# Two attention loops on one Trainium2 core: probability copies cut in half between VectorE and ScalarE, and three steps moved in the order of the engines

## What is computed

```python
for i in range(DEPTH):                                   # DEPTH = 2
    n = rmsnorm(h, attn_norm_g[i])
    m = dsa_mixer(n, ...) if i % 2 == 0 else chunk_band_mixer(n, ...)
    h = h + m @ w_out[i]
    h = h + conv_ffn(rmsnorm(h, ffn_norm_g[i]), ...)

# inside both mixers, per head and block of queries
logits = q @ k.T * scale + bias        # masked keys are -inf
p = softmax(logits)
o = p @ v
```

## Time and profile before

| | |
|---|---|
| median of 3 executions | 3011.78 us |
| lowest and highest | 3011.35 and 3015.06 us |
| the profiled execution | 3010.81 us |
| its span, first to last instruction | 3008.6 us |
| mean granted clock of TensorE | 0.973 |
| TensorE busy | 2792.0 us, 93% |
| VectorE busy | 1525.4 us, 51% |
| ScalarE busy | 1111.2 us, 37% |
| GpSimd busy | 840.1 us, 28% |

### The profile page before, as it was taken

One profiled execution on the slowest core, in us unless ns is written; L12 is line 12 of the kernel. 1 busy time (PEld: TensorE's weight loads), 2 busy tenths in 40 slices (PEclk: granted clock), 3 DMA queues, 4 the chain that ended last, 5 costly groups with the idle time before them and its releaser, 6 DMA issues. The chain is left out here.

```text
span 3008.6 us, 38734 instructions
## 1 busy us (share of the span) xinstructions
PE 2792.0 (93%) x14678; PEld 2388.8 (79%) x14678; DVE 1525.4 (51%) x2431; ACT 1111.2 (37%) x2392; POOL 840.1 (28%) x479
## 2 busy tenths in 40 slices
PE   6797698999999999999989986888999999999999
PEld 5697587887788888888879986777877888888887
DVE  5899665651544444544441113777515444444444
ACT  4677465551322222222245534666413222222221
POOL 4021523202332232232244431111023223232221
PEclk9899799999999999999989998999999999999999
DMA  4110000011211111111031100001012111111111
GB/s 162 42 43 1 25 5 8 14 52 42 71 49 49 42 43 54 42 50 50 12 130 43 43 21 1 12 26 68 8 36 77 50 42 52 45 42 56 49 42 63
DMA packets 38754, 132.43 MB, mean 44 GB/s; under 512 B 4240, under 2 KB 12608, under 8 KB 36960
## 3 DMA queue, kind: packets, MB, share of 16 engines
q1 hardware_dynamic: 38624, 130.68, 13.0%
HBM read 122.22 MB, written 13.69 MB: 45 GB/s over the span
## 5 line engine op out<-in xcount | busy, mean ns | idle before, releaser
L330 PE MATMUL banks<-XH,WH 128*128 128x512 f32 x1408 | 446.1, 397 | 5.3 <-POOL WL L291 4.2
L330 PE MATMUL banks<-XL,WH 128*128 128x512 f32 x1408 | 444.2, 396 | 0.0
L330 PE MATMUL banks<-XH,WL 128*128 128x512 f32 x1408 | 444.1, 396 | 0.0
L291 POOL TENSOR_TENSOR WL<-WR,WH 128x1024 fp32r<-128x1024 f32 x132 | 332.1, 2523 | 389.4 <-ACT WH L245 389.4
L260 ACT ACTIVATE Y<-U,CONVB,CONVW 128x1024 f32<-128x1024 f32 x88 | 109.5, 1244 | 659.7 <-DVE U L386 659.7
L386 DVE TENSOR_TENSOR U<-banks,RB 128x1024 f32<-128x1024 f32 x88 | 107.8, 1225 | 433.8 <-PE banks L330 424.5
L330 PEld LDWEIGHTS banks<-XH,WH 128*128 128x128 f32 x1408 | 265.4, 189 | 70.4 <-POOL WL L291 4.4
L330 PEld LDWEIGHTS banks<-XL,WH 128*128 128x128 f32 x1408 | 265.6, 189 | 64.2
L330 PEld LDWEIGHTS banks<-XH,WL 128*128 128x128 f32 x1408 | 265.3, 188 | 64.2
L376 DVE TENSOR_TENSOR XT<-XT,banks 128x1024 f32<-128x1024 f32 x176 | 214.6, 1219 | 164.7 <-PE banks L346 164.7
L299 POOL TENSOR_TENSOR AL<-Y,AH 128x1024 fp32r<-128x1024 f32 x44 | 106.0, 2410 | 625.5 <-ACT AH L268 625.5
(11 more groups left out here) (225 smaller groups left out, 5462.9 us busy)
## 6 DMA issues: line engine op xcount, KB each, us to landing
WR<-in_ffn SPq DMA_DIRECT2D x132, 512.0 KB, 3.4
QWR<-in_qkv SPq DMA_DIRECT2D x12, 1536.0 KB, 6.7
XT<-in_xT SPq DMA_DIRECT2D x16, 512.0 KB, 7.8
OWR<-in_w_o SPq DMA_DIRECT2D x16, 512.0 KB, 3.2
spill<-XT SPq DMA_DIRECT2D x8, 512.0 KB, 14.6
XT<-spill SPq DMA_DIRECT2D x8, 512.0 KB, 7.1
outT<-XT SPq DMA_DIRECT2D x8, 512.0 KB, 2.6
near<-strip SPq DMA_DIRECT2D x1, 3072.0 KB, 21.3
```

Of the source, the lines that this page charges most:

```text
L291: pool.tensor_tensor(WL[:, ch % RING, :], WR[:, ch % RING, :], WH[:, ch % RING, :].bitcast(F32), ALU.subtract).then_inc(w_lo, 1)
L330: mm = pe.matmul(u[:, h * HALF:(h + 1) * HALF], w[:, ch % RING, db * P:(db + 1) * P], x[:, db, h * HALF:(h + 1) * HALF], start=(db == 0 an ...
```

## The change

It has four parts.

1. **Where the turned blocks go.** A function `cut(n)` says how many of n blocks go to the first bank. In the band it is n up to three blocks, 2 of four and 3 of five; in DSA n up to four, 3 of five, 3 of six, 4 of seven and 4 of eight. `t_first` is signalled after that many blocks.
2. **Who copies how much.** VectorE copies the first bank at its new width, ScalarE the second. In the band ScalarE now copies two of four blocks.
3. **TensorE's order.** `values(g - 1)` stands right behind `turn(g)`, ahead of `logits(g + 3)` and of what goes through bank `TQ`.
4. **VectorE's order.** `output(g // 2 - 1)` stands right behind the copy of unit g, ahead of `row_max(g + 3)` and of `heads_low`.

The diff of the band (that of DSA makes the same moves):

```diff
+        def cut(n):
+            return n if n < 4 else (n + 1) // 2
...
                 if n <= 3 * P:
                     act.wait_ge(t_first, g + 1)
                     act.activation(pt[:, 0:n], TP[0][:, 0:n], ACT.Copy).then_inc(pt_act, 1)
-                elif n > HALF:
+                else:
+                    c0 = cut(blocks(i)) * P
                     act.wait_ge(t_second, seconds_before(g + 1))
-                    act.activation(pt[:, HALF:n], TP[1][:, 0:n - HALF], ACT.Copy).then_inc(pt_act, 1)
+                    act.activation(pt[:, c0:n], TP[1][:, 0:n - c0], ACT.Copy).then_inc(pt_act, 1)
...
+                    bank, seat = divmod(b, cut(n))
+                    mm = pe.transpose(TP[bank][:, seat * P:(seat + 1) * P], PR[:, g % AHEAD, b * P:(b + 1) * P],
                                       c.IDF[:])
-                    if b == min(last, 3):
+                    if b == cut(n) - 1:
                         mm.then_inc(t_first, 1)
...
             for g in range(ALL):
                 turn(g)
+                if g >= 1:
+                    values(g - 1)
                 if g + AHEAD < ALL:
                     logits(g + AHEAD)
                 if tile_of(g) is not None:
                     heads(tile_of(g), rounds_before(g))
                 if output_of(g) is not None:
                     output(output_of(g), rounds_before(g))
-                if g >= 1:
-                    values(g - 1)
...
                     dve.wait_ge(t_first, g + 1)
-                    dve.tensor_copy(PT[:, g % 2, 0:HALF], TP[0][:]).then_inc(pt_dve, 1)
+                    c0 = cut(blocks(i)) * P
+                    dve.tensor_copy(PT[:, g % 2, 0:c0], TP[0][:, 0:c0]).then_inc(pt_dve, 1)
+                if h == 0 and g >= 2:
+                    output(g // 2 - 1)
                 if g + AHEAD < ALL:
                     row_max(g + AHEAD)
                 if tile_of(g) is not None:
                     heads_low(tile_of(g), rounds_before(g))
                 if output_of(g) is not None:
                     output_low(output_of(g), rounds_before(g))
-                if h == 0 and g >= 2:
-                    output(g // 2 - 1)
```

More of the change, by code:

```diff
@@ L586, in seconds_before @@
         def seconds_before(g):
-            return sum(blocks(place(v)[1]) > 4 for v in range(g))
+            return sum(blocks(place(v)[1]) >= 4 for v in range(g))
+        def cut(n):
+            return n if n < 4 else (n + 1) // 2
         def firsts_before(g):
@@ L813, in turn @@
                     pe.wait_ge(pt_dve, firsts_before(g))
-                last = blocks(i) - 1
-                for b in range(last + 1):
-                    mm = pe.transpose(TP[b // 4][:, b % 4 * P:(b % 4 + 1) * P], PR[:, g % AHEAD, b * P:(b + 1) * P],
+                n = blocks(i)
+                for b in range(n):
+                    bank, seat = divmod(b, cut(n))
+                    mm = pe.transpose(TP[bank][:, seat * P:(seat + 1) * P], PR[:, g % AHEAD, b * P:(b + 1) * P],
                                       c.IDF[:])
-                    if b == min(last, 3):
+                    if b == cut(n) - 1:
                         mm.then_inc(t_first, 1)
-                if last >= 4:
+                if n >= 4:
                     mm.then_inc(t_second, 1)
             def acts_before(g):
-                return sum(blocks(place(v)[1]) != 4 for v in range(g))
+                return g
             def values(g):
@@ L1076, in seconds_before, with cut @@
             return sum(place(v)[3] >= 4 for v in range(g))
+        def cut(n):
+            return n if n <= 4 else (n + 1) // 2
         @block.sync
@@ L1142, in _ @@
                     act.wait_ge(t_second, seconds_before(g + 1))
-                    act.activation(pt[:, HALF:n], TP[1][:, 0:n - HALF], ACT.Copy).then_inc(pt_act, 1)
+                    c0 = cut(i + 1) * P
+                    act.activation(pt[:, c0:n], TP[1][:, 0:n - c0], ACT.Copy).then_inc(pt_act, 1)
                 if g + 2 < ALL:
@@ L1258, in turn @@
                 for b in range(i + 1):
-                    mm = pe.transpose(TP[b // 4][:, b % 4 * P:(b % 4 + 1) * P], PR[:, g % AHEAD, b * P:(b + 1) * P],
+                    bank, seat = divmod(b, cut(i + 1))
+                    mm = pe.transpose(TP[bank][:, seat * P:(seat + 1) * P], PR[:, g % AHEAD, b * P:(b + 1) * P],
                                       c.IDF[:])
-                    if b == min(i, 3):
+                    if b == cut(i + 1) - 1:
                         mm.then_inc(t_first, 1)
```

## The result

| | before | with the change |
|---|---|---|
| median | 3013.42 us (4 runs) | 2995.28 us (4 runs) |
| lowest and highest | 3011.35 to 3015.55 | 2994.95 to 2996.10 |
| profiled execution, its span | 3010.81, 3008.6 | 2996.10, 2993.9 |

The ratio is 0.994, with a 95% interval of 0.9923 to 0.9957: 18 us faster. The forecast was 20.7 us faster, and 2990 us. The two profiled executions differ by 14.7 us: that of the kernel before ran 2.6 us under its median, that of the changed kernel 0.8 us over.

A forecast was written before the change was run, and what follows sets the result against it. TensorE was taken to bound the kernel, losing time in the band before the output's transpose, waiting for `MO`. Gains of 14.5 (seven band groups), 1.2 (eighth) and 5 (DSA) made 20.7 us off 3010.81: 2990 us, range 2962 to 3004.

The forecast's parts named there:

- What bounds: In the band TensorE stands still before the output's transpose, where `MO` comes last: 42.9 us in 56 waits.
- What is late next: In the band VectorE's odd-unit copy behind the low parts holds the turn; five-block pairs take 5.46 us, where 5.52 stood.
- The rival of full recovery: Band and DSA: the copy isn't in the way and TensorE becomes the bound; 48 us off, 2963 us; chance 0.12.
- Rule and row: Band copy's start on VectorE: the skill's drain rule gives 5.54 us a pair, the trace's 0.40 us gives 5.46, used.
- Tiles 0 to 2: Band tiles without a VectorE copy: tile 0 loses 0.43 us, tile 1 gains 0.7, tile 2 gains 0.8.
- the rule of thumb: Band tiles 0 to 2: old time, plus values ahead of `heads`, less 0.45 us for `MO`, less the odd unit's values.
- The eighth group: The band's last group prepares no heads; only its few short `MO` waits go, gaining an estimated 1.2 us.
- for ScalarE nothing: The split's added and wider copies cost ScalarE nothing, since it then waits for the later `heads` anyway.
- DSA: DSA's loop gains 5 us from `MO` waits; late `queries` and eased `DUP` waits cancel; bounds -6 to +12.
- no wait for the copy is added: Moving `values(g - 1)` behind `turn(g)` on TensorE adds no copy wait, as the turn already waits for both copies.
- Slower: Rival: in band tiles 3 to 7 ScalarE's exponential falls inside the chain, 35 us lost, 3025 us; chance 0.06.

The follow-up runs named there:

- Experiment 5: Changed kernel, but in the band VectorE writes the low parts of the heads behind the odd unit's copy; 2984.97 us, ratio 0.9895 to the kernel before.
- Experiment 1: Changed kernel without the new split: up to four blocks go to the first bank, copied whole by VectorE; 3002.67 us, ratio 0.9966 to the kernel before.
- experiment 2: Kernel before with the new split of the copies alone, all orders on TensorE and VectorE as before; 3013.10 us, ratio 1.0.
- Experiment 6: Changed kernel, but DSA's groups without queries (2, 4, 6, 7) keep the old TensorE and VectorE orders; 2988.40 us, ratio 0.9908 to the kernel before.
- Experiment 3: Changed kernel, but VectorE makes the output last, as before; TensorE's new order and the split stay; 3246.80 us, ratio 1.0761 to the kernel before.

## Why the prediction was right, and where it was not

**What bounds.** Right. TensorE's standing still before the output's transpose was the loss, and `MO` was what came last.

**What is late next.** Right, and to the digit: 5.46 us for a pair of five blocks, made of the terms that were counted from the earlier trace rows. Tile 4 takes 5.32 us for 5.24: once a group, there, VectorE writes a mask (L923) between the low keys and the copy, which starts 0.54 us behind the low keys and not 0.40. The sum had no term for it. Experiment 5 takes the copy off the chain and gets 5.19, near the 5.22 that the sum gave TensorE alone. Experiment 1 makes the copy 0.13 us longer and gets 0.13 us more a pair. The rival of full recovery was refuted by the same rows; it needed a move that the change doesn't make.

**Rule and row.** The prediction had them differ, but it used only half of the rule. The Trainium skill (VectorE: DVE Perf Modes, The DRAIN you can't avoid) says that the next op does not start until the pipe is empty, and goes on that a next op that is not held starts earlier. The copy starts 0.40 us after the low keys, whose own record is 0.48 us long (1917.37, 1917.77), so the trace agrees with the second half. The sum went by the row, and that was right.

**Tiles 0 to 2.** Right: 0.41 lost, 0.69 and 0.90 gained, for 0.43, 0.7 and 0.8. For tile 2 more was gained than the rule of thumb gave, as said there.

**The eighth group.** The term of 1.2 us was too high (and two waits of 0.77 make 1.5). The first seven groups gained 15.0 us for 14.5, the eighth 0.4. Its pairs of tiles 0 to 6 take 25.53 us against 25.70 before; the `MO` waits went, but the new order costs TensorE some 0.07 us in each long pair.

**The split.** The step "for ScalarE nothing" held: in the pair of tile 5 ScalarE stood idle for 1.02 us before its pass over the heads (1916.00). That the split is worth nothing alone, as experiment 2 shows, had not been asked.

**DSA.** Mis-sized: +5 stood in the sum and 1.7 was measured. What failed is that the sum had no term for the groups that prepare no queries. It let `values` move ahead there for nothing, on the step "no wait for the copy is added". That is true of the copy, but `values` has a second wait, for `MO`, since the output's bank is shared, and in groups 2 and 4 VectorE's variance makes `MO` late. Groups 2, 4 and 6 lost 4.3 us and group 7 another 0.4. Experiment 6 puts the loss of the first three down to the order. Groups 0, 1, 3 and 5 gained 6.5 us. Of that 3.9 lie outside the first pairs of groups 1, 3 and 5, near the 5 for `MO`. In those first pairs the late `queries` and the eased waits for `DUP` were to cancel; group 5's lost 1.0, those of groups 1 and 3 gained 1.8 each. That DSA didn't come out at a loss is owed to these two, and so partly to luck. The range had room for all this (-6 to +12).

**Slower.** The rival's mechanism, the exponential inside the chain, didn't come. In the pair of tile 5 `row_max(g+2)` ended 0.7 us in, as placed, and the exponential 2.0 us in, 1.02 before its engine's next work on the chain. Experiment 3 shows that a far worse loss was near: with one of the two moves missing, 8% slower.

## What to carry to other kernels

When a wait is taken off a chain, write down the next thing that the same engine does after the released work and who waits for it: here a copy of 0.55 us took the wait's place, and moving it was worth another 10.8 us of the band's loop. Moves on two engines that hang together through a shared bank have to be made together; each alone cost 47 and 233 us. An order that pays where an engine has holes can cost where it has none, 4.7 us in four of DSA's groups here, and is better kept out of such stretches.

## What the runs showed of the hardware that I had not expected

Repeated waits of 1.8 us a pair did not only cost themselves (experiment 3): in some stretches behind them the granted clock was mostly at its lower level (0.59 on average over 18 us), and values of five blocks went from 1.23 to 2.23 us. It did not happen everywhere: two of DSA's groups with waits of the same kind were granted 1.00.

Where TensorE has no holes, order by itself had a price here. In DSA's group 6 a pair of six blocks went from 6.39 to 6.48 us with the same work for TensorE, and back to 6.39 with the old order in experiment 6, where the split was still in. From the load of values (four blocks) to the next turn it was 0.85 us before (612.28 to 613.13), and to the logits that now follow it is 0.89 (611.37 to 612.26):

```profile
612.28 0.98 PEld L1274 LDWEIGHTS banks<-QKVB,PT 128*128 128x128 f32 x8
613.13 0.58 PEld L1259 LDWEIGHTS banks<-IDF,PR 128*128 128x128 f32 x5
```

```profile
611.37 0.97 PEld L1287 LDWEIGHTS banks<-QKVB,PT 128*128 128x128 f32 x8
612.26 0.19 PEld L1257 LDWEIGHTS banks<-KH,QS 128*128 128x128 f32 x1
```

The first pair of rows is of the kernel before, the second of the changed one. What in the array makes the difference was not tried.
